# A decoder trunk on one core: a ring for two experts' weights becomes a ring for three, and the groups of rows run in one plain loop

## The reference, cut to what matters

```python
def _moe(x, w_router, b_router, wg, wu, wd):
    ...   # 16 experts in 4 groups; each row takes the best group, then its best 2 experts
    for e in range(N_EXPERTS):
        hid = jax.nn.silu(xt @ wg[e]) * (xt @ wu[e])
        y = y + gates[:, e:e + 1] * (hid @ wd[e])
```

## Time and profile before

| | us |
|---|---|
| median of 3 runs | 1430.92 (1420.81 to 1433.12) |
| the profiled execution | 1430.51 |
| its span | 1428.3 |
| TensorE busy in it | 1075.3 (75%) |
| mixer, layer 0 | about 0 to 268 |
| router and plan, layer 0 | 268 to 322 |
| groups of layer 0 | 322.6 to 596.1 |
| read back, normalise | 597 to 628 |
| mixer, layer 1 | 628 to 1076 |
| router and plan, layer 1 | 1076 to 1123 |
| groups of layer 1 | 1123.8 to 1394.3 |
| read back, normalise, store | 1394 to 1428 |

### The profile page before, as it was taken

The page is one execution under the profiler, slowest core; times in us unless marked ns, Lnnn a source line. Parts: engine busy times, 40 slices in busy tenths (PEclk is TensorE's granted clock), DMA queues, the critical chain, the costliest instruction groups (busy, mean ns, idle before and its releaser), DMA issues.

```text
span 1428.3 us, 21314 instructions
## 1 busy us (share of the span) xinstructions
PE 1075.3 (75%) x8508; PEld 596.0 (42%) x8509; DVE 413.6 (29%) x849; ACT 152.5 (11%) x313; POOL 236.2 (17%) x356
## 2 busy tenths in 40 slices
PE   5995666926489887459999999999895355589870
PEld 4643343413255454234354554544444233245540
DVE  0499543440001110152232433324126000001105
ACT  1012232101001000011101111011001000001000
POOL 1394100120111211101112212111000200111210
PEclk9996666957789999869999999999996677799985
DMA  9601370446999987762553626524225487999873
GB/s 339 231 1 50 111 294 30 153 158 255 410 414 421 422 350 315 284 205 91 189 192 122 212 94 210 194 95 178 89 118 189 165 335 325 372 404 415 341 292 113
DMA packets 81194, 327.68 MB, mean 229 GB/s; under 512 B 7107, under 2 KB 16415, under 8 KB 72805
## 3 DMA queue, kind: packets, MB, share of 16 engines
q1 hardware_dynamic: 59469, 259.70, 46.3%
q0 software_dynamic: 16048, 50.69, 10.3%
q10 hardware_dynamic: 5616, 16.42, 3.3%
HBM read 297.20 MB, written 32.59 MB: 231 GB/s over the span
## 4 chain that ended last, share of the span: by engine, by line
PE 56%; DMA 23%; DVE 13%; issue 3%; POOL 2%; ACT 1%; SPq 1%; ACTq 0%; POOLq 0%; DVEq 0%
DMA ring<-in_w_e_up_dram 16%; PE ps L1651 12%; PE ps L1573 11%; DVE scratch L1308 5%; PE ps L1598 4%; DMA ring<-in_w_e_down_dram 4%; PE ps L1870 4%; PE ps L1970 4%; PE ps L1897 3%; PE ps L1689 2%; PE ps L1883 2%; PE ps L1835 2%; DMA ring<-in_w_in_a_dram 1%; PE ps L1888 1%; PE ps L1934 1%
## 5 line engine op out<-in xcount | busy, mean ns | idle before, releaser
L1573 PE MATMUL ps<-ring,scratch 128*32 128x256 f32 x3840 | 253.8, 425 | 128.2 <-DMA ring<-in_w_e_up_dram 114.2
L1573 PEld LDWEIGHTS ps<-ring,scratch 128*32 128x32 f32 x3840 | 149.3, 122 | 222.4 <-issue 171.9
L1651 PE MATMUL ps<-xT,ring 128*128 128x320 f32 x640 | 187.3, 454 | 3.7 <-DMA ring<-in_w_in_a_dram 2.9
L1651 PEld LDWEIGHTS ps<-xT,ring 128*128 128x128 f32 x640 | 127.0, 200 | 64.3 <-issue 19.6
L1598 PE MATMUL ps<-ring,scratch 128*32 128x256 f32 x1920 | 116.0, 390 | 22.9 <-DMA ring<-in_w_e_down_dram 14.7
L1217 DVE TENSOR_TENSOR scratch<-scratch,ps 64x512 f32<-64x512 f32 x30 | 20.6, 685 | 387.4 <-ACT scratch L837 387.4
L651 POOL DMA_INDIRECT y_quarters<-scratch x60 | 59.2, 987 | 351.9 <-DVE scratch L1223 342.8
L1598 PEld LDWEIGHTS ps<-ring,scratch 128*32 128x32 f32 x1920 | 62.2, 112 | 68.0 <-DMA ring<-in_w_e_down_dram 18.2
L1466 DVE SCALAR_TENSOR_TENSOR scratch<-scratch,ps 128x512 f32<-128x512 f32 x64 | 43.9, 687 | 136.4 <-PE ps L1897 129.3
L1308 DVE SCALAR_TENSOR_TENSOR scratch<-scratch 128x256 f32<-128x256 f32 x120 | 75.6, 705 | 0.0
L1870 PE MATMUL ps<-ring,xT 128*128 128x512 f32 x128 | 57.9, 605 | 0.0
(11 more groups left out here) (298 smaller groups left out, 1044.7 us busy)
## 6 DMA issues: line engine op xcount, KB each, us to landing
ring<-in_w_e_gate_dram SPq DMA_DIRECT2D x32, 2048.0 KB, 13.0
ring<-in_w_e_up_dram SPq DMA_DIRECT2D x32, 2048.0 KB, 17.5
ring<-in_w_e_down_dram SPq DMA_DIRECT2D x32, 2048.0 KB, 16.2
scratch<-in_state_ret_dram POOLq DMA_DIRECT2D x32, 512.0 KB, 5.7
ring<-in_w_in_c_dram SPq DMA_DIRECT2D x8, 2048.0 KB, 13.3
out_ret_sample_dram<-scratch POOLq DMA_DIRECT2D x32, 512.0 KB, 4.4
ring<-in_w_in_a_dram SPq DMA_DIRECT2D x5, 2048.0 KB, 21.6
ring<-in_w_in_c_dram SPq DMA_DIRECT2D x8, 1024.0 KB, 12.0
```

The source lines that it names most:

```text
L1573: ins = pe.matmul(ps[r0:r0 + CHUNK, B_GU + hf, a2 * 256:a2 * 256 + 256], xgT[:, k, c0:c0 + CHUNK], ring[:, slot + j, k * D_FF + n * 256:k ...
L1651: ins = pe.matmul(bank(j)[:, 0:TOK], w[:, k, k0:k0 + P], xT[:, k, :], start=k == 0, stop=k == KD - 1)
```

## The change

The ring gets room for three experts: slots 6 to 8 lie in the scratch memory (`more`), for which the tiles of all stages are laid out anew, and the buffer `yy` of the read back now lies over the rows and hidden values of the groups. Expert e goes to side e mod 3 in layer 0 and to the next but one in layer 1; the semaphores of the slots are shared by both layers. `by_side` holds three copies of a chunk's matmuls in place of two.

The loader asks for nine blocks ahead (the three new slots once the heads are turned in layer 0, once all states are written out in layer 1), then for gate and up of e, then down of e-1. A slot waits for the expert three before. SP's loop becomes straight code.

PE's loop over groups holds a whole group: gate and up of chunks 0, 1 and 2, the turn of half 0, gate and up of chunk 3, down of chunk 0, the turn of half 1, the turn of the next group's rows, down of chunks 1, 2 and 3. No part of a group stands outside the loop. ACT's, DVE's and POOL's loops follow that order. The rows of one group more are gathered and turned than there are (`TABLE_QUADS`), and ACT waits for that turn's copy ahead of the read back. `experts_i` holds four experts in place of six (two operations of DVE less), and one scalar of the plan goes.

The first five states (L765) are asked for behind POOL's part of the experts of layer 0, and `tbc` behind the read back. Of layer 1's weights the first three blocks go to side 1, the next three behind `yy_asked`.

```diff
@@ -351,7 +358,15 @@
 
         w_landed = [sem(f"w_landed{s}") for s in range(RING)]
 
-        e_landed = [[sem(f"e_landed{l}_{s}") for s in range(RING)] for l in range(2)]
+        e_landed = [sem(f"e_landed{s}") for s in range(SLOTS)]
+
+        def side_of(l, e):
+
+            return (e + 2 * l) % 3
+
+        def earlier_turns(l, side):
+
+            return sum(side_of(0, e) == side for e in range(N_EXP)) if l else 0
 
...
                 if j < 2:
...
-            def down_load(l, e, side, turns):
-
-                chunks = sp.value_load(done_i[0:1, bass.ds(e - 1, 1)], min_val=1, max_val=MAX_CHUNKS + 1)
-                s = 3 * side + 2
-                sp.wait_ge(e_landed[l][s], turns * 16)
-                sp.wait_ge(L[l]["y_full"], chunks)
-                load_expert(l, e, 2, s)
-
-            def experts(l):
-                for j, side in ((0, 0), (1, 0), (2, 0), (0, 1), (1, 1), (2, 1)):
-                    await_full(sp, last_in_slot[l][3 * side + j])
-                    load_expert(l, side, j, 3 * side + j)
+                    return gu[e].rearrange("(p k) f -> p (k f)", k=KD)
+                return a["w_e_down"][l, e].rearrange("(j p) d -> p j d", p=P)
+
+            def load_expert(l, e, j):
+
+                s = 3 * side_of(l, e) + j
+                dst = slot(s) if j < 2 else slot(s).rearrange("p (j d) -> p j d", j=KF)
+                sp.dma_start(dst, weights_of(l, e, j)).then_inc(e_landed[s], 16)
+
+            def experts(l, free):
+
+                for s, wait_free in free:
+                    e = [e for e in range(3) if side_of(l, e) == s // 3][0]
+                    if earlier_turns(l, s // 3):
+                        sp.wait_ge(e_landed[s], 16 * earlier_turns(l, s // 3))
+                    wait_free()
+                    load_expert(l, e, s % 3)
                 sp.wait_ge(S["plan_ready"], l + 1)
-                gate_up_loads(l, 2, 0, 1)
-                with sp.Fori(1, N_EXP // 2 - 1) as i:
-                    gate_up_loads(l, i * 2 + 1, 1, i)
-                    down_load(l, i * 2, 0, i)
-                    gate_up_loads(l, i * 2 + 2, 0, i + 1)
-                    down_load(l, i * 2 + 1, 1, i)
-                gate_up_loads(l, N_EXP - 1, 1, N_EXP // 2 - 1)
-                down_load(l, N_EXP - 2, 0, N_EXP // 2 - 1)
-                down_load(l, N_EXP - 1, 1, N_EXP // 2 - 1)
-
+
+                def load_next(e, blocks):
+                    chunks = sp.value_load(done_i[0:1, e - 2:e - 1], min_val=1, max_val=MAX_CHUNKS + 1)
+                    for j in blocks:
+                        s = 3 * side_of(l, e) + j
+                        sp.wait_ge(e_landed[s], 16 * (earlier_turns(l, s // 3) + e // 3))
+                        if j != 1:
+                            sp.wait_ge(L[l]["y_full" if j == 2 else "gu_full"], chunks)
+                        load_expert(l, e, j)
+
+                for e in range(3, N_EXP):
+                    load_next(e, (0, 1))
+                    if e > 3:
+                        load_next(e - 1, (2,))
+                load_next(N_EXP - 1, (2,))
...
@@ -569,7 +577,15 @@
                 await_full(sp, ("SS", g))
                 await_full(sp, ("wT", 2 * g))
                 load_pages(g + 2)
-            experts(0)
+            def used(s):
+                return lambda: await_full(sp, last_in_slot[0][s])
+
+            def heads_turned():
+                for i in range(2):
+                    await_full(sp, ("aoT", i))
+                await_full(sp, ("cT", 2))
+
+            experts(0, [(s, used(s)) for s in range(4)] + [(s, heads_turned) for s in (6, 7, 8)] + [(s, used(s)) for s in (4, 5)])
 
...
                 load_c(n)
 
             sp.wait_ge(S["yy_asked"], 1)
-            for n in (1, 2, 3):
-                sp.wait_ge(e_landed[0][loads[1, n][0]], 16 * N_EXP // 2)
+            for n in range(3, RING):
+                sp.wait_ge(e_landed[loads[1, n][0]], 16 * earlier_turns(1, 0))
                 load_c(n)
             for n in range(RING, 3 * H):
                 load_c(n)
             for n in range(2):
                 for r in range(2):
...
@@ -659,20 +682,18 @@
 
             pool.sem_inc(Q["yb_open0"], 1)
             pool.sem_inc(Q["yb_open1"], 1)
-            pool.wait_ge(S["plan_ready"], l + 1)
-            before_last = pool.value_load(quads_i[0:1, 1:2], min_val=2 * TOK // P - 2, max_val=MAX_QUADS - 2)
+            last = last_quad(pool, l)
             gather(1)
-            with pool.Fori(0, before_last) as i:
+            with pool.Fori(0, last) as i:
                 scatter(i, 0)
                 gather(i + 2)
-                reopen(i, 0)
                 scatter(i, 1)
-                reopen(i, 1)
-            for i in (before_last, before_last + 1):
-                for hf in range(2):
-                    scatter(i, hf)
                 for hf in range(2):
                     reopen(i, hf)
+            for hf in range(2):
+                scatter(last, hf)
+            for hf in range(2):
+                reopen(last, hf)
...
@@ -764,10 +785,9 @@
             def load_state(j):
                 pool.dma_start(s0b[:, j % S0_RING], state(a["state_ret"], SEQ_ORDER[j % DEC_B], j // DEC_B)).then_inc(s0_in[j % S0_RING], 16)
 
-            pool.wait_ge(S["x_done"], 3)
+            experts_pool(pool, 0)
             for j in range(S0_RING):
                 load_state(j)
-            experts_pool(pool, 0)
...
@@ -842,17 +860,14 @@
 
             last = last_quad(act, l)
             turned(0)
-            swish(0, 0)
-            hidden(0, 0)
-            with act.Fori(0, last) as i:
-                swish(i, 1)
+            with act.Fori(0, last + 1) as i:
+                for hf in range(2):
+                    swish(i, hf)
+                    hidden(i, hf)
                 turned(i + 1)
-                hidden(i, 1)
-                swish(i + 1, 0)
-                hidden(i + 1, 0)
-            swish(last, 1)
-            hidden(last, 1)
-
+
+            act.wait_ge(Q["xa_done"], last + 2)
+            act.sem_inc(S["met"], 1)
             act.wait_ge(Q["y_out0"], last * 32 + 32)
...
@@ -1537,15 +1546,19 @@
             def experts_of(i):
 
 
-                code = pe.value_load(experts_i[0:1, bass.ds(i, 1)], min_val=0, max_val=N_EXP ** 6 - 1)
-                return [(e & 1, (e >> 1) * 16 + 16) for e in [(code >> (4 * u)) & 15 for u in range(6)]]
+                code = pe.value_load(experts_i[0:1, bass.ds(i, 1)], min_val=0, max_val=N_EXP ** 4 - 1)
+                out = []
+                for u in range(4):
+                    e = (code >> (4 * u)) & 15
+                    turn = (e * 11) >> 5
+                    out.append((e - turn * 3, turn * 16 + 16))
+                return out
 
             def by_side(side, products):
 
-                with pe.If(side == 0):
-                    products(0)
-                with pe.If(side == 1):
-                    products(3)
+                for e in range(3):
+                    with pe.If(side == e):
+                        products(3 * side_of(l, e), 16 * earlier_turns(l, side_of(l, e)))
 
             def turn_rows(i):
 
...
+                    pe.wait_ge(Q["xa_done"], i + 1)
+                    pe.wait_ge(Q["xd_done"], i + 1)
+                    pe.wait_ge(Q[f"hid_done{hf}"], i + 1)
+                c0 = hf * HALF_ROWS + a2 * CHUNK
+
+                def products(s, base):
+                    for j in range(2):
+                        pe.wait_ge(e_landed[s + j], landed + base)
+                    for k in range(KD):
+                        for j in range(2):
+                            for n in range(2):
+                                r0 = HALF_ROWS * (hf if j else 1 - hf) + n * CHUNK
+                                ins = pe.matmul(ps[r0:r0 + CHUNK, B_GU + hf, a2 * 256:a2 * 256 + 256], xgT[:, k, c0:c0 + CHUNK],
+                                                slot(s + j)[:, k * D_FF + n * 256:k * D_FF + n * 256 + 256], start=k == 0, stop=k == KD - 1)
+                    ins.then_inc(Q["gu_full"], 1)
+
+                by_side(side, products)
 
             def turn_hidden(i, hf):
                 pe.wait_ge(Q[f"hid_done{hf}"], i + 2)
...
@@ -1583,45 +1596,42 @@
                     ins = pe.transpose(ps[:, B_HT + hf, j * HALF_ROWS:(j + 1) * HALF_ROWS], hid[HALF[hf], j * P:j * P + P], ident[HALF[hf], HALF[hf]])
                 ins.then_inc(Q["ht_full"], 1)
 
-            def down(i, hf, experts):
-
-                pe.wait_ge(Q["ht_read"], i * 2 + (hf + 1))
-                pe.wait_ge(Q[f"yd_done{hf}"], i + 1)
-                for a2, (side, landed) in enumerate(experts):
-
-                    def products(slot):
-                        pe.wait_ge(e_landed[l][slot + 2], landed)
-                        for n in range(2):
-                            for j in range(2):
-                                for q in range(4):
-                                    f = 2 * n + j
```

(83 more changed lines are left out.)

87 lines of the change are left out of this document (30 added, 57 removed).

## The result

The changed kernel takes 1628.19 us (median of 4 runs, 1623.17 to 1630.61) where the kernel before takes 1425.87 (4 runs, 1417.84 to 1433.12): a ratio of 1.142, 95% interval 1.134 to 1.150. The forecast was 1578. The profiled execution of the changed kernel has a span of 1628.8 us, that of before 1428.3.

What follows compares the result with a forecast made beforehand. Weight transfers bound the expert stages before; after, PE's refetched loop code would. From 1430.5: +94.5 (layer 0), +51.5 (layer 1), +2 and -1 for small edits gave 1578 us; range for 8 in 10, 1375 to 1640.

Steps and rivals of the forecast that it cites:

- I take the second: PE's expert loop, 9.3 packets: every packet is fetched again each round, 9.5 x 2.2 = 21 us; chance 0.50.
- some 180: Sign on queue q8: code packets in the whole span, 9.5 x 15 plus 35 for the rest, in place of 45.
- holes: Gaps in the expert stages' weight transfers, as at 343 us; remaining ones costed at nothing with three sides.
- Rival 1: PE's expert loop: all code stays on the chip, 25 us a group, transfers decide, 1343 us; chance 0.15.
- Rival 2: PE's expert loop: fixed packet places, part stays, 34 to 38 us a group, 1379 to 1457 us; chance 0.30.
- The proof that ended at 7: PE's old expert loop: the trace shows some 7 packets stay on the chip, none of 10 shown.
- the group: 46 us forecast: PE's time per expert group: 24 us work, 1 us between pieces, 21 us code.
- code and pauses: PE's expert groups: 21 us of refetched code plus 1 us between pieces, per group.
- a rival at 0.05: PE's expert groups: all packets refetched and much work at 1.2 GHz, up to 48 us, above 1640; chance 0.05.
- The bound of 50 us a group: Upper bound for PE's expert groups, 10.3 packets at 2.4 us: +126 us in layer 0, +80 in layer 1.
- the transfers' 93 us: Expert stages by transfers alone: layer 0 ends 43 us earlier, layer 1 50 us earlier.
- The small edits: States and `tbc` moved to the end of layer 0's experts: +2 us; fewer DVE plan operations: -1 us.

Runs made afterwards that it cites:

- e1: Kernel before plus never-run third copies in TensorE's loops: all four places in layer 0, the two down places in layer 1; 1610.7 us.
- e2: Kernel before plus never-run third copies: both gate and up places in layer 0's loop, one down place in layer 1's; 1601.2 us.
- e4: Changed kernel with two experts' room and two copies of each product in place of three; 1533.9 us, ratio 1.076 to the kernel before.
- e6: Kernel before with 25 never-run matmuls ahead of layer 0's loop, both loops moved onto eight packets; 1512.1 us.
- e3: Changed kernel, in layer 1 only one copy of each product, multiplying by columns of xT instead of the expert's blocks; 1504.1 us.
- e8: Kernel before with 60 never-run matmuls ahead of layer 0's loop, both loops moved but again on seven packets; 1419.2 us, ratio 0.996.
- e7: Kernel before with 12 never-run matmuls ahead of layer 0's loop: layer 0's loop on seven packets, layer 1's on eight; 1467.7 us.
- e5: e4 with 28 never-run matmuls ahead of layer 1's loop, moving it from eight packets to seven; 1472.9 us, 1.034 times the kernel before.

## Why the prediction was right, and where it was off

**The step "I take the second" was right.** q8 brought 182 packets where some 180 were forecast, with some luck in the total: 160 came while groups ran and 22 besides, where the forecast had 143 and 35. They came in every turn (10 to 12 in the settled turns of layer 0); "issue" ends PE's pauses; waits for up blocks are gone from the top of the list; the DMA share is below 0.8. The nine blocks were asked for ahead of each layer's groups (the last at 276.93 and 1196.04). Whether holes are left can't be read here, since the transfers wait for PE. The reason given, that a store which gives up the oldest packet keeps nothing of a loop that is too long, fits 9 to 11 packets (e1, e2, after) and eight in e4. It is too strict for eight in e6, where a part stays in some turns. Rival 1 (all stays) and rival 2 (a fixed place, part stays) fall for the changed loop with the 86 and 74 packets of its two layers. Rival 2's sum was not right in itself: 34 to 38 us a group give 1398 to 1458, not 1379 to 1457, so the low end of the range stood too low. No packet count came near that rival.

**The proof that ended at 7 was closer to the limit than it looked.** The prediction read off that a loop on some seven packets stays and left open where above 7 the limit lies. It is 7, and the kernel before stands on it only by its place: its loops end 0.30 and 0.12 packets ahead of the next one. 0.4 packets further on (e6) it was 85 us slower itself.

**The term of the sum that was mis-sized is the group: 46 us forecast, 50.3 and 50.4 measured.** Of its three parts, code and pauses were 21 + 1; PE's idle time is (402.5 - 248.6) / 8 = 19.2 us. That part was right within 3 us, by two errors that nearly cancel: 10.8 packets a group at 1.79 us each in layer 0, where 9.5 at 2.2 were forecast. The work was put at 24 us and is 248.6 / 8 = 31.1. Some 1.5 us of that was there before: 204.2 / 8 = 25.5. The other 5.6 go with the clock, 0.79 in place of 0.90 over the stage: by the clock records of the trace, 13.5 us of a group's work ran at 0.50 in the changed kernel and 4.2 us before. At twice the time for the same work, that is 4.7 of the 5.6 us. The prediction left the clock outside its sum. It had seen that matmuls ran slower after a long idle time, but gave it to a rival at 0.05 since pieces between 2 us pauses ran at full speed. The pauses of the new loop are not all of 2 us: several packets in a row make one of 6 or 9 us, and behind those the pieces run slower (32 products of down take 3.64 us at 521.60, behind 6.04 us of idle time and at a granted clock of 0.50). e1 and e3 are the checks: with fetches in the old order the group's work is 255.9 / 8 = 32.0 us at 0.79, without them in the new order 25.3 at 0.89. Over 15 groups the miss is 34.5 + 30.6 = 65 us; the mixer's 15 us the other way leave the 50 us between 1578 and 1628. The bound of 50 us a group, worked out for 10.3 packets at 2.4 us and work at full clock, was reached for another reason: cheaper packets and slower work. So it is in part luck that 1628 still lies inside the range, 12 us from its end.

**Of the transfers' 93 us, layer 1's part was there, but the changed kernel can't reach it.** In e3 layer 1's groups take 224.0 us where the forecast for the transfers alone was 1344 - 1123.8 = 220.2, 46.5 us less than before. Layer 0's 43 us were not measured by themselves. In the changed kernel these gains lie beneath PE's code.

**The small edits** were right: the read back grew by 1.9 us, forecast 2. The first product comes at 325.1, 2.5 us later, forecast nothing. In e3, with the same code up to there, it came at 322.3, and in e1, with the old code, at 325.4, so no effect of the change shows.

**The mixer's -15 us were not forecast and no run shows them to be an effect of the change.** The stage from 628.3 to 4 us ahead of layer 1's groups, in the kernel before and in e8, which has the same code there:

```profile
628.00:1120.00 492.00, 454.29 (x1506) 225.87 (x1506) 157.28 (x360) 47.00 (x75) 70.17 (x91) 0.91 0.42 145
```

```profile
628.00:1108.00 480.00, 442.44 (x1506) 221.96 (x1506) 156.92 (x360) 47.02 (x75) 70.15 (x91) 0.93 0.43 148
```

PE's work for the same 1506 products is 454 us in one execution and 442 in another at a slightly higher clock. By the stage table's measure the kernel before has 495.5 us; the nine other profiles have 480.3 to 487.0, and five of them (e1, e2, e6, e7, e8) hold the old code there. So the one profile of the kernel before is the long one, and the changed kernel's 480.3 is no gain that the edit made.

**Open.** A kernel with three slots whose loops lie on seven packets was not built: its twelve copies take 9.53. What e3's layer 1 gained, without the expert's weights in its products, stays a bound. What the plain order costs with two slots was not traced beyond the waits of e5. Why a loop on eight packets keeps a part in some turns was not settled.

## What to carry to other kernels

Count the instructions of a loop on TensorE before unrolling it further: every `If` copy is code, run or not, and here one more copy at each of four places, never run, cost 128 us in a stage of 273 (e1). Look at the instruction queue of the profile by stretch: packets inside a loop's later turns are the sign, and "issue" as the releaser of PE's pauses is the other. If a loop is near the limit, look at its place too: dead code ahead of it can push it over, or pull it back.

## What the runs showed of the hardware that was not expected

A loop's place in the program matters as well as its length: 1,655 instructions on seven packets of 16 KB ran without a fetch after the second turn (12 packets while a layer's groups ran), the same instructions 103 further on lay on eight and brought 49, for 85 us (e6), and 243 further on ran free again (e8). In layer 0 of the changed kernel a fetched packet costs twice: 1.79 us of PE's idle time on average, and the work behind the pauses, which went from 25.5 to 31.1 us a group at a granted clock of 0.79 in place of 0.90.
